# Six byte offsets per layer for the split-weight slots of both ffn stages, in a two-block fp32 transformer kernel on one Trainium2 core

## The reference, cut to what matters

```
h  = h + mix @ w_out[l]                                  # 1024 x 1024
hn = rms_norm_2(h, ffn_norm[l])
gu = hn @ w_gate_up[l]                                   # 1024 x 5632
h  = h + (silu(gu[..., :D_FF]) * gu[..., D_FF:]) @ w_down[l]   # 2816 x 1024
```

## The kernel before

| | slot 0 | slot 1 | slot 2 |
|---|---|---|---|
| tiles as moving operand | 10 | 11 | 9 |
| tiles as stationary operand | 15 | 14 | 15 |

## Time and profile before

### The profile page before, as it was taken

One profiled execution on the slowest core, in us unless ns is written; L12 is line 12 of the kernel. 1 busy time (PEld: TensorE's weight loads), 2 busy tenths in 40 slices (PEclk: granted clock), 3 DMA queues, 4 the chain that ended last, 5 costly groups with the idle time before them and its releaser, 6 DMA issues. The chain is left out here.

```text
span 3453.0 us, 44411 instructions
## 1 busy us (share of the span) xinstructions
PE 3084.7 (89%) x17561; PEld 2186.2 (63%) x17561; DVE 1385.0 (40%) x2258; ACT 1115.5 (32%) x1938; POOL 251.2 (7%) x278
## 2 busy tenths in 40 slices
PE   7999999999698887788787698889999998889999
PEld 5777888878533333333333485768888775778887
DVE  6872566654430000000000467553332467543332
ACT  4672666762200000000000435432222336332222
POOL 0000332210000000000000000300000000300000
PEclk9999999999799999999999799999999998999999
DMA  6332222234699999999998520023333420023332
GB/s 135 88 79 76 77 67 66 73 99 128 252 383 427 425 426 426 425 426 426 426 426 358 158 74 13 6 92 92 97 98 104 93 57 1 22 88 98 98 98 92
DMA packets 361295, 612.37 MB, mean 177 GB/s; under 512 B 73952, under 2 KB 308224, under 8 KB 336384
## 3 DMA queue, kind: packets, MB, share of 16 engines
q1 hardware_dynamic: 351152, 598.72, 47.8%
q0 software_dynamic: 9216, 8.42, 0.7%
q10 hardware_dynamic: 720, 2.36, 0.2%
HBM read 605.23 MB, written 23.07 MB: 182 GB/s over the span
## 5 line engine op out<-in xcount | busy, mean ns | idle before, releaser
L1868 PE MATMUL ex_up<-ex_W,ex_XT 128*64 128x512 f32 x1024 | 259.1, 664 | 79.0 <-DMA ex_W<-in_w_expert_up_dram 79.0
L249 ACT ACTIVATE f_hi<-f_raw 128x1024 fp32r<-128x1024 f32 x148 | 156.6, 1059 | 521.4 <-PE ff_bk L309 520.3
L1868 PE MATMUL ex_gp<-ex_W,ex_XT 128*64 128x512 f32 x1024 | 239.9, 622 | 57.5 <-DMA ex_W<-in_w_expert_gate_dram 56.1
L307 PE MATMUL ff_bk<-h_b_hi,f_hi 128*128 128x512 f32 x704 | 276.4, 393 | 2.8 <-DVE h_b_lo L3840 2.8
L308 PE MATMUL ff_bk<-h_b_lo,f_hi 128*128 128x512 f32 x704 | 275.9, 392 | 0.0
L309 PE MATMUL ff_bk<-h_b_hi,f_lo 128*128 128x512 f32 x704 | 275.7, 392 | 0.0
L258 DVE TENSOR_TENSOR f_lo<-f_raw,f_hi 128x1024 fp32r<-128x1024 f32 x148 | 180.4, 1222 | 210.3 <-ACT f_hi L249 210.0
L1911 DVE TENSOR_TENSOR ex_hid<-ex_sg,ex_up 128x512 f32<-128x512 f32 x32 | 22.0, 687 | 589.7 <-PE ex_up L1868 589.7
L1897 PE MATMUL ex_yp<-ex_W,ex_hT 128*64 128x512 f32 x1024 | 228.5, 598 | 32.3 <-ACT ex_hT L1929 16.4
L1868 PEld LDWEIGHTS ex_up<-ex_W,ex_XT 128*64 128x64 f32 x1024 | 92.0, 152 | 245.3 <-issue 245.3
L1868 PEld LDWEIGHTS ex_gp<-ex_W,ex_XT 128*64 128x64 f32 x1024 | 87.5, 143 | 208.9 <-issue 207.1
(11 more groups left out here) (612 smaller groups left out, 6316.6 us busy)
## 6 DMA issues: line engine op xcount, KB each, us to landing
ex_W<-in_w_expert_up_dram SPq DMA_DIRECT2D x64, 2048.0 KB, 37.8
ex_W<-in_w_expert_down_dram SPq DMA_DIRECT2D x64, 2048.0 KB, 38.8
ex_W<-in_w_expert_gate_dram SPq DMA_DIRECT2D x64, 2048.0 KB, 37.8
b_raw<-in_w_in_dram SPq DMA_DIRECT2D x88, 512.0 KB, 4.0
f_raw<-in_w_gate_up_dram SPq DMA_DIRECT2D x88, 512.0 KB, 3.9
f_raw<-in_w_down_dram SPq DMA_DIRECT2D x44, 512.0 KB, 3.6
m_raw<-in_w_in_dram SPq DMA_DIRECT2D x20, 512.0 KB, 4.0
m_early<-in_w_in_dram SPq DMA_DIRECT2D x20, 512.0 KB, 4.1
```

Of the source, the lines that this page charges most:

```text
L249: a.activation(self.hi[n % self.SLOTS][:, at], self.raw[n % self.RAW][:, at], ACT.Copy).then_inc(self.cast, 1)
L307: pe.matmul(out, a[0], b[0], start=first, stop=False)
L1868: ins = pe.matmul(ps[part[e], :], XT[b][:, q, part[e]], row_view(slots[e], KD)[:, q, :], start=(q == 0), stop=(q == KD - 1))
```

## The change

`Stream` gets a new argument `apart`, six byte offsets, zero for all other streams. The two ffn streams pass one tuple each. In place of six allocations there is one, `slots`, 512 bytes larger when the offsets are not zero, and the six slots are laid over it at 4096-byte distances plus their offset: the multiple of 32 in the address, the rest as a first column of the slice. The first three offsets are those of the hi slots, the last three those of the lo slots. Slots get the letters a, b, c in place of 0, 1, 2 in their names. What lies behind the slots in these two stages (fT and the small tiles) moves up by 512 bytes. The raw slots, the instructions, their order and their semaphores are the same.

```diff
-    def __init__(self, k, ctx, tag, tiles, early=None):
-        self.tiles, self.issued, self.tag, self.early = tiles, 0, tag, early
+    def __init__(self, k, ctx, tag, tiles, early=None, apart=(0,) * 6):
+        self.tiles, self.issued, self.tag, self.early, self.apart = tiles, 0, tag, early, apart
...
-        self.hi = [k.sb(f"{self.tag}_hi{i}", [P, 1024], F32R, ctx) for i in range(self.SLOTS)]
-        self.lo = [k.sb(f"{self.tag}_lo{i}", [P, 1024], F32R, ctx) for i in range(self.SLOTS)]
+        at = k.next_left()
+        k.sb(f"{self.tag}_slots", [P, (6 * 4096 + 512 * any(self.apart)) // 4], F32, ctx)
+        names = "abc" if any(self.apart) else "012"
+        slot = lambda part, i, at, n: k.over(f"{self.tag}_{part}{i}", [P, 1024 + n % 32 // 4], F32R, at + n // 32 * 32)[:, n % 32 // 4:]
+        self.hi = [slot("hi", names[i], at + 4096 * i, self.apart[i]) for i in range(self.SLOTS)]
+        self.lo = [slot("lo", names[i], at + 4096 * (3 + i), self.apart[3 + i]) for i in range(self.SLOTS)]
...
-        W = Stream(k, c0, f"f{l}", ffn_tiles(g("w_out"), g("w_gate_up"), g("w_down")))
+        W = Stream(k, c0, f"f{l}", ffn_tiles(g("w_out"), g("w_gate_up"), g("w_down")), apart=APART[l])
...
+APART = ((4, 8, 16, 28, 52, 496), (180, 192, 200, 208, 216, 480))
```

## The result

The changed kernel takes 3467.88 us (median of six runs, 3464.32 to 3475.53), the kernel before 3453.03 beside it (six runs, 3446.4 to 3459.9). The ratio is **1.0046, 95% interval 1.0035 to 1.0057**: slower by 0.46%, some 15 us. The forecast of no change was wrong: 3454.0 us was 14 us short. The time is inside the range only because the range had been drawn up to the first rival, whose 3469 it meets within about 1 us.

A forecast was written before the change was run, and what follows sets the result against it. The prediction took PE's pace, 0.227 us a matmul in the ffn stages, as the bound. All terms summed to 0 against 3454.89 us profiled, given as 3454.0 us in terms of the median; range 3447 to 3472 us.

The forecast's parts named there:

- the first rival: Ffn stages: operand distances off multiples of 512 bytes make PE's pace irregular, 5.1 ns a matmul, 15 us, 3469 us; chance 0.19.
- its own sign: The prediction counts as wrong if the two ffn stages together change by more than 7 us.
- (d): PE streams moving weights off the grid, 1192 times: bounds 0 to 242 us, taken as 0 because of L2307.
- (c): PEld loads stationary weights off the grid, 1768 times: up to 37 ns more fits inside a 227 ns step, taken as 0.
- the count: Matmuls touched in the ffn stages, those with weights off the 32-byte grid: 2960 of 3552.
- (a): ACT writes hi off the grid in the ffn stages: at most 4 ns a slot, nothing against its 260.7 us idle.
- (b): DVE reads hi and writes lo off the grid: upper bound 4.6 us for two layers, taken as 0.
- (e): fT, small tiles and row loads move by 512 bytes, distances to h and raw slots stay multiples of 512: cost 0.
- The line rule: Skill's penalty for new 16-byte SBUF lines: 1.7 ns for each of 896 moving reads, sum 1.5 us higher.
- The other rivals: Lost full rate: 3553 or 3696 us, chance 0.08, smaller losses 0.02; faster, streams kept apart: 3416 or 3441 us, chance 0.09.

The follow-up runs named there:

- experiment 1: Changed kernel with all offsets 0 in layer 0 (larger allocation and overlay kept) and 32 in layer 1: 3464.46 us against 3451.84 for the kernel before.
- experiment 4: Changed kernel with all six offsets 128 in layer 0 and 256 in layer 1: 3461.14 us against 3451.84 for the kernel before.
- experiment 3: Changed kernel with all six offsets 4 in layer 0 and 8 in layer 1: 3478.75 us against 3451.84 for the kernel before.
- experiment 11: Changed kernel with all twelve offsets 32, four executions: 3473.34 us, ratio 1.0055 to the kernel before.
- experiment 10: Changed kernel with all twelve offsets 256, eleven executions: 3453.05 us against 3454.74 for the kernel before, ratio 0.9996.
- experiment 2: Changed kernel with all six offsets 16 in layer 0 and 64 in layer 1: 3469.23 us against 3451.84 for the kernel before.
- experiment 5: Changed kernel with slots and fT both moved 4 bytes in layer 0 and 192 in layer 1, h unmoved: 3472.28 us against 3452.6 for the kernel before.
- experiment 8: Changed kernel with slots and fT both moved 8 bytes in layer 0 and 16 in layer 1, h unmoved: 3472.27 us against 3452.08 for the kernel before.
- experiment 6: Changed kernel with offsets 0 and the 96-column tile's pieces 512 bytes apart in place of 384: 3450.22 us against 3452.6 for the kernel before.
- experiment 7: Changed kernel with offsets hi 128, lo 512 in layer 0 and hi 0, lo 128 in layer 1: 3468.21 us against 3452.6 for the kernel before.
- experiment 9: Changed kernel with offsets hi 16, lo 496 in layer 0 and hi 240, lo 272 in layer 1: 3468.4 us against 3452.08 for the kernel before.

## Where the prediction was right and where wrong, point by point

**By its own sign the prediction is wrong.** It named a change of the two stages together by more than 7 us; they are 16.5 us longer. The steps that failed are (d), then (c) and the count.

**(a), (b), the splits on ACT and DVE: right.** 1.06 and 1.22 us are unmoved, the upper bound of 4.6 us was not touched.

**(c), the weight loads: wrong.** The step said that 37 ns of slack inside a 227 ns step would cover them. The loads are recorded 187 to 195 ns long, much as before, but the step beside them is not: 230.3 and 232.4 ns in the gate parts, 9 to 10 us over 2112 matmuls. The slack in the recorded duration of a load did not cover a load that is read at another distance from the stream. Experiments 1 and 4 show the distance alone doing this, at 32 and 128 bytes and on the grid.

**(d), the moving stream: wrong**, and it was the step that the forecast hung on. Taking the low end because of L2307 carried a result from a pass of half the rate to one of the full rate. The row gives durations too, 587 to 612 ns, a spread in which 5 to 7 ns can't be seen. At 1.2 GHz nine steps of the stage take 0.427 each, with nothing but columns; at 2.4 GHz 13 ns are added. That was the sign that at full rate something beside the columns is at work, and the nearest row had to be sought there. The runs bear this out: with offsets that cost the moving weights 6 to 10 ns a step at 2.4 GHz, steps at 1.2 GHz stay at 427 (experiments 3 and 11). Measured, a moving slot costs 5.5 ns in layer 0 and 7.2 in layer 1, 9 us over 1440 matmuls by the mean step. The full range of bounds held, the choice within it did not.

**(e), the shift of fT and the allocation: right** (experiment 1, layer 0; experiment 10).

**The count: wrong.** 2960 matmuls were put down as touched, those off the 32-byte grid. The slots at 192 and 480 are no multiple of 256 bytes away either, and offsets on the grid cost (experiments 1, 2, 4, 11). What these two pay in the changed kernel can't be read off, since they are mixed with others.

**The first rival was right in the main in mechanism, and in size, on a witness that was only partly one.** It named the distance, 5.1 ns a matmul and 15 us; measured are 3.6 to 7.2 ns over all 3552, and 15 us. It left out the start off the grid, which costs by itself (experiments 5 and 8). Its 5.1 ns came from the 96-column tile, and experiment 6 shows that only some 2 ns of these are distance. That the sum hits within about 1 us is luck in part: the price was higher than its source bears, the count was too low, and of the 19 us by mean step only 15 reach the span, with fewer steps at 1.2 GHz and a rest of the program that is 2 us shorter.

**The line rule.** The Trainium skill, "Advanced Engine Details and Errata", section "SBUF Cachelines", states 16-byte lines and a penalty for going to a new one. My reading of it, one line more a stream at 1.7 ns, pointed to slower and was far too low. With fT following, starts off the 32-byte grid cost 5 to 11 ns, also at 16 bytes, where no 16-byte line is cut. There the measurement decides: an extra 16-byte line is not what costs.

**The other rivals.** No slot runs at 0.43 us a step at the 2.4 GHz level, so no rate is lost; no part of any setting had a mean step under 226.7 ns, so none of the distances tried gives back the 13 ns.

## What to carry to other kernels

In a PE-bound part of float32r matmuls, keep the start addresses of both operands on the 32-byte grid and a multiple of 256 bytes apart; the layout costs nothing, and 32 bytes off it cost these stages 2.5% (experiment 11). When the mean distance of starts in a steady part is above that of another part with the same shapes, look at addresses too, and not only at waits: here the counts and the waits of PE stayed as they were, and durations hardly told. And a row that shows no cost at half the rate bounds nothing at the full one.

## What the runs showed of the hardware that was not expected

At the 2.4 GHz level the pace of float32r matmuls depends on where the two operands lie relative to each other, with a period of 256 bytes: 226.7 to 227.0 ns at 0 and 256, 232.4 at 128. At the 1.2 GHz level it doesn't: 427 ns with every offset. It is not the sum of two separate prices: with 4 bytes on both sides the step (237.7 ns) is as long as with 4 on one (237.3). The regular pace breaks for neighbours too (experiment 7), and the same addresses gave 226.7 and 232.6 ns in two kernels (slot c, experiment 9). Not settled: why 64 costs 6.6 ns with stationary weights and 2.0 with moving ones, why 192 costs only 2.2, and why slot c of layer 0 kept the regular pace in the changed kernel and not in experiment 9. The thought that weight load and moving stream, both read from SBUF, get in each other's way would fit the distance, the missing excess at 1.2 GHz and the neighbours of experiment 7; but no run took one of the two away, so it is argued and not shown.
